# Three nested loops around the token block of a mixture-of-experts kernel: block 0; blocks 1 and 2; blocks 3 to 8

## The reference, cut to what matters

```python
def moe(h, w_router, b_router, w1, b1, w2, b2):            # h: 288 x 1024
    logits = h @ w_router + b_router
    top_v, top_i = lax.top_k(logits, 4)
    gates = jax.nn.softmax(top_v, axis=-1)
    ...                                                    # tokens sorted by expert, in blocks
    def expert_block(xb, e):
        a = xb @ w1[e] + b1[e]                             # 1024 -> 2048
        x_glu = jnp.minimum(a[:, :D_FF], 7.0)
        x_lin = jnp.clip(a[:, D_FF:], -7.0, 7.0)
        mid = x_glu * jax.nn.sigmoid(1.702 * x_glu) * (x_lin + 1.0)
        return mid @ w2[e] + b2[e]                         # 1024 -> 1024
    out = out.at[row_tok].add(ys * row_gate[:, None])
```

## Time and profile before

| what | value |
|---|---|
| median of 3 runs | 1331.16 us |
| the runs | 1328.86, 1331.16, 1510.05 us |
| profiled execution | 1338.79 us, of which 1337.0 us span |
| TensorE matmul busy | 1151.3 us (86%), mean granted clock 0.955 |
| VectorE, ScalarE, GpSimd busy | 575.9, 223.2, 82.1 us |
| moved by DMA | 445.26 MB, 333 GB/s over the span |
| chain that ended last | PE 56%, DVE 11%, DMA 10%, issue 8%, SP queue 6%, DVE queue 5% |

### The profile page before, as it was taken

One profiled execution on the slowest core, in us unless ns is written; L12 is line 12 of the kernel. 1 busy time (PEld: TensorE's weight loads), 2 busy tenths in 40 slices (PEclk: granted clock), 3 DMA queues, 4 the chain that ended last, 5 costly groups with the idle time before them and its releaser, 6 DMA issues.

```text
span 1337.0 us, 25940 instructions
## 1 busy us (share of the span) xinstructions
PE 1151.3 (86%) x8837; PEld 450.1 (34%) x8838; DVE 575.9 (43%) x1306; ACT 223.2 (17%) x428; POOL 82.1 (6%) x189
## 2 busy tenths in 40 slices
PE   5998878979888998989898985998989878988984
PEld 4765544433222332323232321233333222332321
DVE  5999744444233344334333422243334233343433
ACT  3103423111111111111111111011111110111112
POOL 2278200000000000000000000000000000000000
PEclk9999899959999999989999999899999989999997
DMA  8416683840999969995999999969996999699993
GB/s 244 159 62 193 211 309 135 301 186 0 390 422 421 422 263 424 422 422 225 424 421 422 421 423 421 422 278 422 422 418 246 422 422 416 285 422 422 422 420 138
DMA packets 77999, 445.26 MB, mean 333 GB/s; under 512 B 16592, under 2 KB 17424, under 8 KB 26736
## 3 DMA queue, kind: packets, MB, share of 16 engines
q1 hardware_dynamic: 77968, 444.87, 82.4%
HBM read 442.33 MB, written 2.51 MB: 333 GB/s over the span
## 4 chain that ended last, share of the span: by engine, by line
PE 56%; DVE 11%; DMA 10%; issue 8%; SPq 6%; DVEq 5%; ACT 1%; POOL 0%; ACTq 0%
PE ps L1531 21%; PE ps L1517 10%; SPq L447 6%; PE ps L1547 5%; PE ps L1540 5%; DMA uni<-in_w_moe_dram 4%; DMA ring<-in_w_moe_dram 4%; PE ps L1559 3%; PE ps L1432 2%; DMA mixer<-in_w_moe_dram 2%; PE ps L1555 1%; PE ps L1572 1%; DVEq L311 1%; DVEq L303 1%; DVEq L315 1%
## 5 line engine op out<-in xcount | busy, mean ns | idle before, releaser
L1531 PE MATMUL ps<-ring,uni 128*32 128x512 f32 x2496 | 286.4, 595 | 9.4 <-DMA ring<-in_w_moe_dram 9.1
L1100 DVE TENSOR_TENSOR x<-x,ps 128x1024 f32<-128x1024 f32 x158 | 186.7, 1208 | 9.9 <-PE ps L1517 7.5
L1517 PE MATMUL ps<-uni 64*128 64x512 f32 x624 | 174.0, 664 | 4.5 <-issue 3.2
L1121 DVE TENSOR_SCALAR uni<-ps 128x256 f32<-128x256 f32 x51 | 21.7, 425 | 338.4 <-PE ps L1531 338.4
L1547 PE MATMUL ps<-uni 128*32 128x256 f32 x1224 | 87.3, 424 | 76.3 <-issue 55.0
L1531 PEld LDWEIGHTS ps<-ring,uni 128*32 128x32 f32 x2496 | 80.0, 110 | 200.0 <-issue 178.2
L1540 PE MATMUL ps<-ring,uni 128*32 128x512 f32 x768 | 90.1, 597 | 23.1 <-DVE uni L1130 16.5
L730 ACT ACTIVATE uni<-uni 128x256 f32<-128x256 f32 x51 | 21.2, 416 | 514.8 <-DVE uni L1121 514.8
L1517 PEld LDWEIGHTS ps<-uni 64*128 64x128 f32 x624 | 55.0, 199 | 101.8 <-issue 95.4
L1547 PEld LDWEIGHTS ps<-uni 128*32 128x32 f32 x1224 | 39.6, 118 | 139.1 <-issue 92.7
L730 ACT ACT_TABLE_LOAD x51 | 65.4, 1283 | 81.7 <-issue 81.4
(11 more groups left out here) (356 smaller groups left out, 1169.3 us busy)
## 6 DMA issues: line engine op xcount, KB each, us to landing
ring<-in_w_moe_dram SPq DMA_DIRECT2D x258, 1024.0 KB, 19.8
tmp<-in_w_moe_dram SPq DMA_DIRECT2D x42, 1024.0 KB, 21.3
w_glu<-in_w_moe_dram SPq DMA_DIRECT2D x21, 1024.0 KB, 24.2
mixer<-in_w_moe_dram SPq DMA_DIRECT2D x21, 1024.0 KB, 24.8
accT<-in_w_moe_dram SPq DMA_DIRECT2D x21, 1024.0 KB, 24.1
uni<-in_w_moe_dram SPq DMA_DIRECT2D x21, 1024.0 KB, 25.5
ring<-in_w_in_dram SPq DMA_DIRECT2D x4, 2048.0 KB, 13.8
ring<-in_cache_k_dram SPq DMA_DIRECT2D x8, 1024.0 KB, 5.2
```

Source lines behind the costliest of these rows:

```text
L1100: tt(rows(t), rows(t), ps[0:TILES[t][1], b0:b0 + 2, :], ALU.add).then_inc(S["acc"], 1)
L1517: ins = mm(ps[:, b0 + c, :], selT[rows, P * t:P * t + P], y[rows, :], start=True, stop=True)
L1531: ins = mm(hidden(q), xe[:, k % 2, quarter(k // 2)], columns(slot(turn, k), q), start=False, stop=(k == 7), skip_group_check=True)
```

## The change

The loops `o` and `c` of three become three nested loops over token offsets, each with a guard. The outermost, `p`, takes 0 and 32. For `p` = 0 each inner loop has one trip (block 0). For `p` = 32 the middle one, `o`, takes 32 and 64; with `o` = 32 the innermost covers blocks 1 and 2, with `o` = 64 blocks 3 to 8. The bounds of the two inner loops are computed in registers. All three engines get the new control; the bodies, the waits, the order of the blocks and SyncE's stream stay as they are.

```diff
-                with eng.Fori(0, 3) as o:
-                    with eng.If(count > o * (3 * CAP)):
-                        with eng.Fori(0, 3) as c:
-                            with eng.If(count > o * (3 * CAP) + c * CAP):
-                                n = eng.snap(done, min_val=0, max_val=NEXP * CHUNKS)
-                                block_of(n, turn, name, before, o * (3 * CAP) + c * CAP)
-                                eng.reg_add(done, done, 1)
+                with eng.Fori(0, 2 * CAP, CAP) as p:
+                    with eng.If(count > p):
+                        with eng.Fori(p, 2 * p + CAP, CAP) as o:
+                            with eng.If(count > o):
+                                with eng.Fori(2 * o - p, 6 * o - 4 * p + CAP, CAP) as c:
+                                    with eng.If(count > c):
+                                        n = eng.snap(done, min_val=0, max_val=NEXP * CHUNKS)
+                                        first = nc.s_assert_within(c, 0, CHUNKS * CAP - CAP, ...)
+                                        block_of(n, turn, name, before, first)
+                                        eng.reg_add(done, done, 1)
```

More of the change, by code:

```diff
@@ L312, in expert @@
                 name = expert_at(eng, e) if named else None
-                with eng.Fori(0, 3) as o:
-                    with eng.If(count > o * (3 * CAP)):
-                        with eng.Fori(0, 3) as c:
-                            with eng.If(count > o * (3 * CAP) + c * CAP):
-                                n = eng.snap(done, min_val=0, max_val=NEXP * CHUNKS)
-                                block_of(n, turn, name, before, o * (3 * CAP) + c * CAP)
-                                eng.reg_add(done, done, 1)
+                with eng.Fori(0, 2 * CAP, CAP) as p:
[5 more added lines that the diff above has]
+                                        n = eng.snap(done, min_val=0, max_val=NEXP * CHUNKS)
+                                        first = nc.s_assert_within(c, 0, CHUNKS * CAP - CAP, skip_runtime_bounds_check_because="p, o, c of the three loops give 0; 1, 2; 3 to 8 times CAP")
+                                        block_of(n, turn, name, before, first)
+                                        eng.reg_add(done, done, 1)
             with nc.Fori(0, NEXP // TURNS, engines=[eng.engine], hint_back_edge=eng is nc.tensor) as g:
```

## The result

The changed kernel takes 1347.08 us (1346.59 to 1350.52, four runs) against 1332.06 us before: 1.0108 of the time, 95% interval 1.0088 to 1.0127. Run again beside later experiments it gave 1346.61 us and 1.0087 (1.0070 to 1.0103). The ratio is taken over undisturbed runs alone; one of the four before took 1510.05 us. The forecast was 1329.2, range 1320 to 1339. It is slower by 12 to 15 us; rival B (1336) and rival C (1366 to 1401) pointed that way. The profiled execution took 1350.52 us, 1348.7 of it span, 11.7 more than the span before.

The account below looks back on a forecast made before the run. Bound by the weight stream at a fixed rate, with TensorE counting ahead of its restarts. Start +0.3, first expert +0.1, e5, e17, e25 +1.5 each, e9 -2.9, e21 -1.8, tail -2.2: -2.0 us, 1329.2 us, range 1320 to 1339.

Parts of the forecast that it names:

- rival B: Crossing from block 0 to 1 in three-block experts: register bounds as dear as loop entries; +5 us, 1336; chance 0.25.
- rival C: Control steps on the path: longer control no longer fits, so code loads each turn; 35 to 70 us more; chance 0.04.
- The step that failed: Change of expert after two or three blocks: one failing guard fewer against the same additions, 0 to 0.3 us less.
- the crossing: Control from block 0 to 1 inside an expert: 0.9 us becomes 2.4, exposing 1.5 in each of e5, e17, e25.
- Start and tail: First block: one loop more to enter, 0.3 us later; after the last block: fewer failing guards, 2.2 us less.
- rival A: Crossing stays as short as 1.2 us and the clock holds after shorter idles: -9 us, 1322; chance 0.19.
- The gains at e9 and e21: Stream restarts at these experts come 2.9 and 1.8 us earlier, from shorter expert changes capped by late last pieces.
- The view of the path: Whole kernel: last stream restart, rest at fixed rate, tail; TensorE's time counts only ahead of a restart.
- the paragraph on the price of a branch: Failing trips: taken branch 222 ns in the rows, about 108 on the skill page; the trace's 0.80 us a trip stands.

Follow-up runs that it names:

- e5, e17: Not a run: an expert of three blocks in the kernel, whose third block restarts the weight stream.
- e6: Not a run: the expert after e5; idle before its first gather shows the cost of a change after three blocks.
- e18: Not a run: the expert that follows e17 in the kernel.
- the seventh experiment: Single loop over the token count, no guards, plus an empty four-trip loop on TensorE after each block, against the kernel before: 1339.44 us, 1.0043.
- e25: Not a run: an expert of three blocks that restarts the weight stream; in the changed kernel its last piece was late by only 0.17 us.
- the ninth experiment: Three loops with the corrected guard on VectorE and ScalarE, single loop over the count on TensorE alone, against the kernel before: 1327.80 us, 0.9952.
- e9, e21: Not a run: an expert of three blocks that restarts the weight stream; its last piece had slack before the change.
- e12: Not a run: one of the kernel's experts, processed in numbered order.
- the second experiment: Changed kernel with its last range cut to blocks 3 to 5, three failing trips in place of six: 1335.99 us, 1.0016 of the kernel before.
- third experiment: Kernel before with its two guarded loops replaced by one loop over the loaded count, without guards: 1325.37 us, 0.9933.

## Why the prediction was wrong

**The step that failed** is "After two or three blocks one guard fails fewer (0.8) against the same additions: 0 to 0.3 us." For three blocks it is wrong. It counts the middle guard at 64 as failing for every expert of fewer than four blocks (only so are there 39 failing guards); that guard passes from 65 tokens on. In its place come six trips of 0.84 us: the idle after three blocks is 4.5 to 4.9 us longer where a gain of 0 to 0.3 was forecast. After two blocks it is 0 to 0.1 us shorter, within the forecast. Two of these changes, e5 to e6 and e17 to e18, lie on the path. Taking the trips away gave back 1.0108 − 1.0045 of the time before, 8 us, by the first comparison, or 1.0087 − 1.0045, 6 us, by the second.

**A term too small: the crossing.** Its place and its control time were right (2.1 us measured, 2.4 forecast), and so was the rule for when it shows: behind a last piece for which TensorE's stream had to stop, as the seventh experiment shows in both directions. Its price was not. The prediction gave 1.5 us, all of it idle, and no slow start at the crossing; it is 2.7 in e5 and 2.6 in e17, of which 1.6 and 1.5 are the slow start, and 1.0 in e25. The two slow gathers in the earlier trace rows stood behind 2.64 and 3.17 us of idle. At the crossing 1.05 us was enough where waits for pieces of 1.4 us came just ahead, and not where they were short (e25 here, four crossings of the seventh experiment). With the guard corrected this term is most of what keeps the kernel 6 us above the time before, where the forecast was 2 us below: with TensorE's crossing short again (the ninth experiment) it is 6 us below.

**Start and tail.** The tail's 2.2 us came out as 2.2 (3.21 to 1.01 us of idle), and 1.8 more from the clock, which only rival A had (as 1.3). The start's 0.3 us cannot be told in the scatter of some 3 us of what comes before.

**The gains at e9 and e21.** The mechanism held: one-block changes fell by 1.76 us, and what arrived was to be capped by the slack of 4.4 and 3.3 us. These two were well sized: from the third block of e5 to the last piece in e9's first block the kernel with the corrected guard, which had to wait for that piece, took 4.2 us less than the kernel before, and from e17 to e21 3.4 less. With the six trips in front the gain never reached the cap (neither crossing waited for its last piece), and the steps were +0.9 and +1.9 instead of −2.9 and −1.8. With the guard corrected the cap did bind, and the exposed crossing with its slow start ate more than half of what it let through.

**A term that was missing.** The late start of e6 also frees its slots late, and the stream pauses a second time, the 387, 408, 390 and 393 of the page. It is 2.3 us between e25 and the last product, by the 393, and 1.1 at e17.

**The rivals.** B had the sign and the place of a part of it, the crossing, with the wrong reason: register bounds were not dear, 0.1 to 0.2 us each by the stream's rows. C did not happen; the sum of control fits, and from 375 to 1290 us the data queue's row is the only one in the changed kernel, as in the earlier trace rows (packets, MB, share):

```profile
q1 hardware_dynamic: 48520, 353.33, 93.2%
```

The view of the path, by which microseconds count only ahead of a restart, is borne out: 31 freed changes of expert gave 9 us, not 50 or more. Its own figure for them, 12, was too high.

**A working that does not come out.** In the paragraph on the price of a branch six branches, each 114 ns shorter than the 222 ns named there, make 0.7 us and not 1.1. No term of the sum rests on it.

## What to carry to other kernels

Run the control by hand for each size of input that occurs, and count passing and failing guards at the boundaries of the ranges; a guard should test the first value that its loop will use, or better be the loop's own bound. Then place each microsecond of control: it is free where the engine's stream runs ahead of its queue, and dear directly behind a wait for data, where the queue is empty and the clock may fall too. Where one engine and a stream of transfers take turns to limit, removing a delay can uncover another.

## What the runs showed of the hardware

- TensorE's granted clock fell to 0.50 (1.2 GHz) for the start of an expert behind 10 of the 17 idles of 2.5 us and more in the kernel before, and in the changed one also behind an idle of 2.31 us (e12). It did so after only 1.05 us where waits for data of 1.4 us came just ahead (seven of eight crossings in the seventh experiment), and not after the same idle without such waits (none of four). In the second experiment e5's crossing started slow with 0.12 us of idle behind waits of 1.3 and 1.4 us: there the clock had fallen before the crossing. A slow start cost 1.5 us from gather to first product (5.3 in place of 3.8). With one matmul of 1.1 us placed in the gap four crossings of five started normally.
- A failing trip of a loop on TensorE's stream took 0.84 us with a guard and 0.38 us without, on VectorE's 0.64 with one. On TensorE about half of the 0.84 us are its two taken branches, 211 to 225 ns each by their own duration; on VectorE a branch has 56 ns. The Trainium skill, page "Advanced Engine Details and Errata", section "Sequencer and Instruction Queues", has about 108 ns for a compare-and-branch; the runs do not agree with that for a taken one.
- TensorE's control behind a block began 2.55 us before the next gather could start where the weights were early, and 0.9 us before it where the last piece had to be waited for (kernel before and third experiment). This is the whole cover that a crossing has.
- A loop whose end is a loaded register (0, 32, ... below the count, which is at least 1) needs no guard. It left no idle at 45 of the 50 boundaries between blocks, and 0.1 to 0.7 us at the five others, all behind late weights.
